# Channel norms of a two-block kernel: sums in four column strips of 128 columns, a reciprocal and a root on 128 columns, and the factor spread by TensorE into PSUM

## The chip, the cores and the metric

One core of one Trainium2 chip runs the whole program. The metric is the device time of one execution in microseconds. The kernel before took 2011.86 us (median of 3 runs, 2007.55 to 2015.01); the profiled execution is one more run, of 2005.91 us, and its span in the profile is 2004.1 us.

## What is computed

Two transformer-like blocks over 512 tokens with 1024 channels, in fp32. The first has a mixer out of a state-space part (SSD) and an RWKV part and a gated feed-forward layer; the second has a modulated mixer of three branches and a hierarchical mixture of experts. The change touches only norms over the channels:

```python
def _rms_norm(x, g):
    xf = x.astype(jnp.float32)
    y = xf * lax.rsqrt(jnp.mean(xf * xf, axis=-1, keepdims=True) + NORM_EPS)
    return (y * g.astype(jnp.float32)).astype(x.dtype)

xn = _rms_norm(h, pre_mix_norm[l]);  proj = xn @ w_in[l]        # pre_mix
y = y.reshape(b, T, SSD_GROUPS, SSD_D // SSD_GROUPS)            # ssd0, ssd1: two groups of 256
y = y * lax.rsqrt(jnp.mean(y * y, axis=-1, keepdims=True) + NORM_EPS)
h = h + _rms_norm(mix, post_mix_norm[l])                        # post_mix
hn = _rms_norm(h, pre_ffn_norm[l])                              # pre_ffn
h = h + _rms_norm(f, post_ffn_norm[l])                          # post_ffn
h = rms_norm(x, g_norm1[l]) * (1.0 + sc1) + sh1                 # sum_1 (second block)
v = layer_norm(v, ln_g, ln_b)                                   # gmlp_var, 512 channels
```

## The kernel before

All activations lie transposed: channels on the 128 partitions, the 512 tokens along the columns, so a row of 1024 channels is eight tiles of 128x512 (`res` is the residual, `xn` the normed one). Every engine has its own program, written out by hand, and semaphores order them; nothing is scheduled by a tool. TensorE's program (from L382) is a list of matmuls in a fixed order. PSUM has eight banks of 512 columns. `open_(what, k, b)` (L392) makes TensorE wait until the former user of bank b has been released, and gives the bank to a new one; `close` tells that it is full; the reader waits with `filled` and releases it with `freed`. So a bank that one reader holds stops TensorE at the next `open_` of this bank, and everything behind that in its program.

A norm over channels takes these steps on three engines:

1. An engine squares each tile (VectorE in pre_mix, ssd, post_mix and gmlp_var, ScalarE in the others), one semaphore count for each.
2. `norm_sum` (L410): one fp32 matmul for each square, a 128x128 block of ones against the tile's 512 columns, all into bank 4. Each of the 128 rows of the result holds the sum over all channels for 512 tokens.
3. `invert_variance` (L1515), on VectorE: `tensor_scalar` from PSUM to `v_tmp` (mean plus epsilon), which releases the bank, then `reciprocal`. Both are 128x512. `v_tmp` and `v_rs` are the halves of the buffer `tiny`.
4. `rstd` on ScalarE (L1151): `Sqrt` of `v_tmp` into `v_rs`, 128x512, recorded at line L1149.
5. VectorE uses `v_rs` as the second tensor of `scalar_tensor_tensor` (the helper `stt`, L1513): tile times gain times factor.

Two functions do step 5 for eight tiles. `scaled_parts` (L1530) makes the input of a projection: `stt` for tile k; ScalarE's `round_hi` (L1170) rounds it into the high part; VectorE subtracts the two for the low part (`in_lo`, `in_ff_lo`), two tiles behind; TensorE's projection begins with tile 0's low part. `add_normed` (L1826) multiplies a tile by gain and factor and adds it to the residual, one tile behind, and ScalarE squares the new residual for the next norm (`squares_of_x`, L1159).

Helpers give the line of many operations: `tt`, `ts` and `stt` are L1507, L1510 and L1513 in the profile, `mm` is L386, `tr` L390.

The places around the norms in TensorE's program: after the "mix" projection (L784) come the sums for post_mix, then `last_modulation(0)`, then the sums for pre_ffn, then the first feed-forward matmuls. `last_modulation` (L469) needs two weight units of 1 MB, a and b: for each, eight matmuls of a 128x32 stationary block, in four column strips of 32, by 256 columns (`rows_of_unit`, L455), an evacuation by ScalarE (`last_mod_rows`), and column matmuls into bank 7. After the feed-forward layer the same follows for post_ffn, `last_modulation(1)` and sum_1. Then two `bias_row` matmuls (L838, 4 output rows by 512 columns, banks 4 and 5), and the "p2" projection of the second block (L840).

Weights come through a ring of two slots (`stream`, L2393): SyncE loads a unit once the unit two before it is used up, which the first instruction on the next unit tells. GpSimd splits each half unit into a high and a low part (L2325 `tensor_scalar`, L2332 `tensor_tensor`), both in SBUF, and waits for the unit's load and for a free slot of the parts.

## Time and profile before

| what | value |
|---|---|
| median of 3 runs | 2011.86 us (2007.55 to 2015.01) |
| the profiled execution, its span | 2005.91 us, 2004.1 us |
| busy: TensorE matmuls, VectorE, ScalarE, GpSimd | 90%, 62%, 24%, 34% |
| TensorE's granted clock, mean of the span | 0.926 of full |
| `reciprocal` on 128x512 in `invert_variance` | 8 times, 26.8 us |
| ScalarE's `Sqrt` on `tiny` | 8 times, 5.0 us |

The rows below have the form: start, duration, engine, line, operation, output<-inputs, shapes, count, and in brackets the idle time before and what ended it. TensorE's fp32 matmuls show as two records each, and a row that merges n records runs from the first start to the last end, so the time from one to the next is less than a record's own length. PE is TensorE, PEld its weight loads, DVE VectorE, ACT ScalarE, POOL GpSimd, SP SyncE.

### The profile page before, as it was taken

The page shows a single profiled execution, that of the slowest core. Times are in us where ns is not written, and L with a number is a line of the kernel's source. Part 1 is how long each engine was busy: PE and PEld are TensorE (multiplying, and loading weights), DVE is VectorE, ACT ScalarE, POOL GpSimd, SP SyncE. Part 2 cuts the span into 40 slices and gives each one's busy share as a digit, 9 for nine tenths or more (in the row PEclk, how much of TensorE's full clock was granted, in tenths as well). Part 3 has the DMA queues.
Part 4 walks back from the last instruction along what each step waited for, and adds up shares of the span by engine and source line. Part 5 has one row for each costly group of instructions (what it writes and reads, how often), then busy time and mean ns, then how long its engine had stood idle before and what let it go on. Part 6 is the DMA issues. An engine that isn't in the chain of part 4 may idle for free.

```text
span 2004.1 us, 28891 instructions
## 1 busy us (share of the span) xinstructions
PE 1805.5 (90%) x11642; PEld 1377.2 (69%) x11642; DVE 1235.2 (62%) x1605; ACT 490.5 (24%) x734; POOL 684.2 (34%) x383
## 2 busy tenths in 40 slices
PE   5999858888969999999889999999898997799998
PEld 4888536766737777777558788876676775566665
DVE  6959366653468888888640385838634544467664
ACT  2121324432021010001221111212143003354443
POOL 2665000001415666666246554005433663000000
PEclk9999679998979999999989999569999999899999
DMA  5221321121114222322212221002311225588884
GB/s 199 86 103 63 117 94 45 51 102 44 64 63 158 90 99 84 104 84 86 82 64 94 79 81 64 1 1 85 100 63 43 85 99 217 200 352 335 321 327 176
DMA packets 34067, 230.49 MB, mean 115 GB/s; under 512 B 4132, under 2 KB 4388, under 8 KB 8232
## 3 DMA queue, kind: packets, MB, share of 16 engines
q1 hardware_dynamic: 30240, 214.48, 29.6%
q10 hardware_dynamic: 2136, 10.24, 1.4%
q0 software_dynamic: 1584, 4.21, 0.6%
q8 instruction: 84, 1.38, 0.3%
q14 instruction: 23, 0.19, 0.0%
HBM read 220.98 MB, written 9.50 MB: 115 GB/s over the span
## 4 chain that ended last, share of the span: by engine, by line
PE 74%; DVE 15%; ACT 4%; DMA 4%; issue 3%; POOL 0%; SPq 0%; DVEq 0%; ACTq 0%; POOLq 0%
PE psum L386 72%; DVE arena L1513 4%; DVE arena L1507 3%; DMA arena<-units 2%; ACT arena L1149 2%; PE psum L390 2%; DVE arena L1510 1%; DVE tiny L1521 1%; ACT L1149 1%; DVE residual L1507 1%; DMA weight_ring<-units 1%; DVE expert_lo L1507 1%; ACT expert_hi L1149 0%; ACT tiny L1149 0%; DMA arena<-x 0%
## 5 line engine op out<-in xcount | busy, mean ns | idle before, releaser
L1149 ACT ACTIVATE arena<-psum 128x512 f32<-128x512 f32 (+4 forms) x295 | 149.3, 521 | 896.2 <-PE psum L386 779.6
L386 PE MATMUL psum<-arena 64*64 64x64 f32 (+5 forms) x2908 | 262.3, 282 | 37.6 <-DVE arena L1507 23.9
L386 PEld LDWEIGHTS psum<-arena 64*64 64x64 f32 (+3 forms) x2908 | 184.4, 166 | 98.3 <-issue 43.9
L386 PE MATMUL psum<-normed_hi,w_in_hi 128*128 128x512 f32 x512 | 205.1, 401 | 12.6 <-DVE in_lo L1507 8.3
L386 PE MATMUL psum<-normed_hi,w_in_lo 128*128 128x512 f32 x512 | 203.5, 397 | 0.0
L386 PE MATMUL psum<-in_lo,w_in_hi 128*128 128x512 f32 x512 | 200.5, 392 | 0.0
L1513 DVE SCALAR_TENSOR_TENSOR arena<-arena,fixed_data 128x512 f32<-128x512 f32 x134 | 188.8, 1409 | 13.5 <-DVE arena L1510 0.2
L1507 DVE TENSOR_TENSOR arena<-arena,psum 128x512 f32<-128x512 f32 (+2 forms) x200 | 110.9, 589 | 134.1 <-PE psum L386 85.5
L2332 POOL TENSOR_TENSOR w_ff_lo<-weight_ring,w_ff_hi 128x1024 fp32r<-128x1024 f32 x66 | 167.0, 2530 | 5.5
L2332 POOL TENSOR_TENSOR w_in_lo<-weight_ring,w_in_hi 128x1024 fp32r<-128x1024 f32 x64 | 163.8, 2560 | 5.3
L386 PE MATMUL psum<-arena,fixed_data 128*128 128x512 f32 (+10 forms) x424 | 135.9, 487 | 30.5 <-DVE arena L1507 20.8
L1507 DVE TENSOR_TENSOR arena<-arena 128x512 f32<-128x512 f32 (+3 forms) x200 | 144.7, 735 | 13.4 <-PE psum L386 5.2
L386 PE MATMUL psum<-normed_hi,w_ff_hi 128*128 128x512 f32 x352 | 139.3, 396 | 8.2 <-DVE in_ff_lo L1507 8.2
L2325 POOL TENSOR_SCALAR w_in_hi<-weight_ring 128x1024 fp32r<-128x1024 f32 x64 | 73.0, 1141 | 203.0 <-PE psum L386 165.1
L2325 POOL TENSOR_SCALAR w_br_hi<-weight_ring 128x1024 fp32r<-128x1024 f32 x44 | 46.6, 1059 | 276.1 <-PE psum L386 159.2
L386 PE MATMUL psum<-in_ff_lo,w_ff_hi 128*128 128x512 f32 x352 | 140.7, 400 | 0.0
L386 PE MATMUL psum<-normed_hi,w_ff_lo 128*128 128x512 f32 x352 | 140.4, 399 | 0.0
L2325 POOL TENSOR_SCALAR w_ff_hi<-weight_ring 128x1024 fp32r<-128x1024 f32 x66 | 74.7, 1132 | 177.1 <-PE psum L386 151.9
L386 PEld LDWEIGHTS psum<-normed_hi,w_in_hi 128*128 128x128 f32 x512 | 96.4, 188 | 42.5 <-issue 14.5
L2325 POOL TENSOR_SCALAR w_out_hi<-weight_ring 128x1024 fp32r<-128x1024 f32 x8 | 8.9, 1112 | 335.2 <-PE psum L386 333.6
L386 PEld LDWEIGHTS psum<-in_lo,w_in_hi 128*128 128x128 f32 x512 | 96.8, 189 | 23.0
L2332 POOL TENSOR_TENSOR w_br_lo<-weight_ring,w_br_hi 128x1024 fp32r<-128x1024 f32 x44 | 110.0, 2499 | 3.7
(226 smaller groups left out, 3564.6 us busy)
## 6 DMA issues: line engine op xcount, KB each, us to landing
weight_ring<-units SPq DMA_DIRECT2D x124, 1024.0 KB, 4.9
arena<-units SPq DMA_DIRECT2D x55, 1024.0 KB, 7.5
normed<-units SPq DMA_DIRECT2D x20, 1024.0 KB, 8.6
slots<-arena ACTq DMA_DIRECT2D x7, 516.0 KB, 5.1
arena<-slots SPq DMA_DIRECT2D x7, 516.0 KB, 5.7
fixed_data<-fixed ACTq DMA_DIRECT2D x1, 2944.0 KB, 12.0
arena<-x SPq DMA_DIRECT2D x4, 512.0 KB, 5.9
arena<-bias_rows ACTq DMA_DIRECT2D x2, 896.0 KB, 5.9
```

The source lines that it names most:

```text
L386: return nc.tensor.matmul(o, l, r, start=start, stop=stop)
L390: return nc.tensor.transpose(o, i, C("ident", k, 0, k))
L1149: return nc.scalar.activation(o, i, func, **kw)
L1507: return V.tensor_tensor(o, a, b, op)
L1510: return V.tensor_scalar(o, a, s1, s2, op0) if op1 is None else V.tensor_scalar(o, a, s1, s2, op0, op1)
L1513: return V.scalar_tensor_tensor(o, a, s1, b, op0, op1)
L1521: V.reciprocal(v_tmp, v_tmp).then_inc(sem("variance_inverted"), 1)
L2325: first = nc.gpsimd.tensor_scalar(hi, raw, 1.0, 1.0, ALU.mult, ALU.mult)
L2332: nc.gpsimd.tensor_tensor(lo, raw, hi.bitcast(F32), ALU.subtract).then_inc(sem("split_ready"), 1)
```

## The change

The sums of steps 2 to 4 are kept on 128 columns instead of 512. `token_sums` replaces `norm_sum` for the eight norms: for each square it does four matmuls of a 128x32 block of ones, one for each quarter j of 128 tokens, which write columns 0 to 127 of PSUM rows 32j to 32j+31. `tensor_scalar`, `reciprocal` and `Sqrt` work on 128x128. `spread_rs` is new on TensorE: it waits for the root and does four 128x128 matmuls, whose stationary block is one column of the identity repeated 128 times, so that row 32j of `v_rs` comes out on all partitions, in columns 128j on; the result is ("rs", what), in bank 4 (5 and 6 for ssd). VectorE's `stt` read it from PSUM, and the last of them releases the bank; what waited for its own semaphore count now waits for this release. In gmlp_var the spread stands one weight unit after the sums, and the two units behind the sums are given one by one. `gmod` is computed ahead of the factor of sum_1 instead of after it. The sums `sum_bonus`, `sum_y` and `gmlp_mean` stay as they were.

```diff
+            def token_sums(what, srcs, ready, b=4):
+
+                o = open_(what, 0, b)
+                for k, src in enumerate(srcs):
+                    pe.wait_ge(*ready(k))
+                    for j in range(4):
+                        last = mm(o[32 * j:32 * j + 32, 0:P], C("ones", P, 0, 32), src[:, j * P:(j + 1) * P],
+                                  k == 0, k == len(srcs) - 1)
+                close(last, what)
+
+            def spread_rs(what, b=4):
+
+                n_rs[0] += 1
+                pe.wait_ge(sem("rstd_ready"), n_rs[0])
+                o = open_(("rs", what), 0, b)
+                for j in range(4):
+                    last = mm(o[:, j * P:(j + 1) * P], C("ident", P, 32 * j, 32 * j + 1).to_broadcast([P, P]), v_rs[:, 0:P])
+                close(last, ("rs", what))
...
-            norm_sum("sum_pre_mix", [A(SQ + k * T) for k in range(KT)], C("ones"), lambda k: (sem("sq_pre_mix"), k + 1))
+            token_sums("sum_pre_mix", [A(SQ + k * T) for k in range(KT)], lambda k: (sem("sq_pre_mix"), k + 1))
+            spread_rs("sum_pre_mix")
...
-            pe.wait_ge(sem("ssd_out_ready"), 4)
+            pe.wait_ge(sem("ssd_out_ready"), 2)
+            for g in range(2):
+                emptied(pe, ("rs", f"sum_ssd{g}"))
...
             sums("sum_post_mix", sq8, "sq_post_mix")
+            spread_rs("sum_post_mix")
             last_modulation(0)
             sums("sum_pre_ffn", sq8, "sq_pre_ffn")
+            spread_rs("sum_pre_ffn")
...
             sums("gmlp_var", [A(g_SQ + k * T) for k in range(4)], "sq_gmlp")
-            project("p2", 2, w_in2, in2, 18)
+            project("p2", 1, w_in2, in2, 18)
+            spread_rs("gmlp_var")
+            project("p2", 1, w_in2, in2, 20)
...
-                f(v_rs, v_tmp, ACT.Sqrt).then_inc(sem("rstd_ready"), 1)
+                f(v_rs[:, 0:P], v_tmp[:, 0:P], ACT.Sqrt).then_inc(sem("rstd_ready"), 1)
...
-                V.tensor_scalar(v_tmp, PSB[bank_of(what, k)], scale, add, ALU.mult, op1).then_inc(freed(what, k), 1)
+                V.tensor_scalar(v_tmp[:, 0:P], PSB[bank_of(what, k)][:, 0:P], scale, add, ALU.mult, op1).then_inc(freed(what, k), 1)
                 emptied(dve, what, k)
-                V.reciprocal(v_tmp, v_tmp).then_inc(sem("variance_inverted"), 1)
+                V.reciprocal(v_tmp[:, 0:P], v_tmp[:, 0:P]).then_inc(sem("variance_inverted"), 1)
...
-                dve.wait_ge(sem("rstd_ready"), n_rstd[0])
+                filled(dve, ("rs", what))
+                return PSB[bank_of(("rs", what))]
...
-                        stt(tiles.raw(k), res[:, k, :], gain(k), v_rs, ALU.mult, ALU.mult).then_inc(sem("scaled"), 1)
+                        stt(tiles.raw(k), res[:, k, :], gain(k), rs, ALU.mult, ALU.mult)\
+                            .then_inc(sem("scaled") if k < KT - 1 else freed(("rs", what)), 1)
...
-                        stt(src(k), src(k), S(gain, k), v_rs, ALU.mult, ALU.mult).then_inc(sem("term_ready"), 1)
+                        stt(src(k), src(k), S(gain, k), rs, ALU.mult, ALU.mult)\
+                            .then_inc(sem("term_ready") if k < KT - 1 else freed(("rs", what)), 1)
```

Three places of TensorE's program show what moves. In the rows, `arena,fixed_data` is squares against ones, `tiny,fixed_data` the spread, `weight_ring,smalls` the rows of a modulation unit. First, the end of the "mix" projection, before:

```order
L386 MATMUL psum<-y_lo,w_out_hi 128x512
L386 MATMUL psum<-arena,fixed_data 128x512 [waits sq_post_mix,bank4_free]
L386 MATMUL psum<-arena,fixed_data 128x512 [waits sq_post_mix] x7
L386 MATMUL psum<-weight_ring,smalls 32x256 [waits bank5_free,weights0_loaded]
L386 MATMUL psum<-weight_ring,smalls 32x256 x7
```

and with the change, from the last of the eight squares on:

```order
L386 MATMUL psum<-arena,fixed_data 32x128 [waits sq_post_mix]
L386 MATMUL psum<-arena,fixed_data 32x128 x3
L386 MATMUL psum<-tiny,fixed_data 128x128 [waits bank4_free,rstd_ready]
L386 MATMUL psum<-tiny,fixed_data 128x128 x3
L386 MATMUL psum<-weight_ring,smalls 32x256 [waits bank5_free,weights0_loaded]
L386 MATMUL psum<-weight_ring,smalls 32x256 x7
```

The spread, which waits for the root, stands ahead of the modulation. Second, sum_1 and the bias rows (`fixed_data 4x512`) ahead of the "p2" projection, before:

```order
L386 MATMUL psum<-arena,fixed_data 128x512 [waits sq_1,bank4_free]
L386 MATMUL psum<-arena,fixed_data 128x512 [waits sq_1] x7
L386 MATMUL psum<-fixed_data 4x512 [waits bank4_free]
L386 MATMUL psum<-fixed_data 4x512 [waits bank5_free]
L386 MATMUL psum<-normed_hi,w_in_hi 128x512 [waits h_ready,bank0_free,split_ready]
```

and with the change, from the last square on:

```order
L386 MATMUL psum<-arena,fixed_data 32x128 [waits sq_1]
L386 MATMUL psum<-arena,fixed_data 32x128 x3
L386 MATMUL psum<-tiny,fixed_data 128x128 [waits bank4_free,rstd_ready]
L386 MATMUL psum<-tiny,fixed_data 128x128 x3
L386 MATMUL psum<-fixed_data 4x512 [waits bank4_free]
L386 MATMUL psum<-fixed_data 4x512 [waits bank5_free]
L386 MATMUL psum<-normed_hi,w_in_hi 128x512 [waits h_ready,bank0_free,split_ready]
```

The wait for bank 4 ahead of the first bias row was one for the `tensor_scalar` of sum_1; now it is one for the last reader of its spread factor. Third, the two ssd norms, with the change:

```order
L386 MATMUL psum<-arena,fixed_data 32x128 [waits sq_ssd,bank6_free]
L386 MATMUL psum<-arena,fixed_data 32x128 x3
L386 MATMUL psum<-arena,fixed_data 32x128 [waits sq_ssd]
L386 MATMUL psum<-arena,fixed_data 32x128 x3
L386 MATMUL psum<-tiny,fixed_data 128x128 [waits bank5_free,rstd_ready]
L386 MATMUL psum<-tiny,fixed_data 128x128 x3
L386 MATMUL psum<-tiny,fixed_data 128x128 [waits bank6_free,rstd_ready]
L386 MATMUL psum<-tiny,fixed_data 128x128 x3
```

Both sums stand ahead of both spreads, each norm in a bank of its own.

## Rows read from the trace of the kernel before

**Rows 1.** The page, part 4: share of the last-ending chain by engine.

```profile
PE 74%; DVE 15%; ACT 4%; DMA 4%; issue 3%; POOL 0%; SPq 0%; DVEq 0%; ACTq 0%; POOLq 0%
```

**Rows 2.** The chain of waits, 555 to 610 us: start, duration, what.

```profile
565.29 3.36 DVE tiny L1521
...
568.67 0.64 ACT tiny L1149
...
569.34 1.42 DVE normed L1513 x2
...
570.75 0.60 DVE residual L1507
571.35 0.66 DVE normed L1513
...
577.86 2.75 DVE residual L1507
...
588.91 0.70 DVE tiny L1519
```

**Rows 3.** The timeline, 557 to 566 us, all engines.

```profile
557.49 7.03 PE L386 MATMUL psum<-arena,fixed_data 128*128 128x512 f32 x16
...
564.45 1.07 PE L386 MATMUL psum<-weight_ring,smalls 128*32 128x256 f32 x16
564.56 0.69 DVE L1519 TENSOR_SCALAR tiny<-psum 128x512 f32<-128x512 f32 x1 [5.55 <-PE psum L386]
```

**Rows 4.** VectorE's groups by form: names, shapes, count, busy us, mean ns, idle.

```profile
L1521 DVE RECIPROCAL tiny<-tiny 128x512 f32<-128x512 f32 x8 | 26.8, 3353 | 0.3
...
L1513 DVE SCALAR_TENSOR_TENSOR arena<-arena,fixed_data,psum 128x512 f32<-128x512 f32 x16 | 11.9, 744 | 10.6 <-ACT arena L1149 6.9 <-PE psum L386 3.1
...
L1513 DVE SCALAR_TENSOR_TENSOR arena<-residual,smalls,tiny 128x512 f32<-128x512 f32 x8 | 5.8, 745 | 0.0
...
L1507 DVE TENSOR_TENSOR arena<-psum,arena 128x128 f32<-128x128 f32 x4 | 1.2, 290 | 5.5 <-PE psum L386 5.5
...
L1807 DVE RECIPROCAL smalls<-smalls 128x32 f32<-128x32 f32 x1 | 0.4, 353 | 0.0
```

**Rows 5.** ScalarE's groups by form.

```profile
L1149 ACT ACTIVATE smalls<-smalls 128x32 f32<-128x32 f32 x2 | 0.5, 229 | 8.7 <-DVE smalls L1807 5.1 <-DVE smalls L1999 3.6
```

**Rows 6.** The timeline of TensorE, 1156.5 to 1176 us.

```profile
1157.37 0.39 PE L386 MATMUL psum<-fixed_data 128*128 128x128 f32 x2
...
1157.82 0.39 PE L386 MATMUL psum<-fixed_data 128*128 128x128 f32 x2
```

**Rows 7.** The timeline, 562 to 608 us: modulation unit b, its columns, GpSimd's first split.

```profile
569.93 1.93 PE L386 MATMUL psum<-weight_ring,smalls 128*32 128x256 f32 x16 [4.40 <-DMA weight_ring<-units]
...
571.79 1.87 PE L386 MATMUL psum<-smalls,arena 128*128 128x1 f32 x8
...
576.14 1.18 POOL L2325 TENSOR_SCALAR w_ff_hi<-weight_ring 128x1024 fp32r<-128x1024 f32 x1 [25.22 <-DMA weight_ring<-units]
```

**Rows 8.** Windows: busy us of PE, PEld, DVE, ACT, POOL, granted clock, DMA share, GB/s.

```profile
26.00:28.00 2.00, 0.00 (x0) 0.00 (x0) 2.00 (x1) 0.00 (x0) 0.00 (x0) 1.00 0.00 0
...
573.00:586.00 13.00, 9.46 (x17) 4.00 (x17) 12.47 (x12) 4.04 (x7) 7.95 (x4) 0.76 0.42 153
```

**Rows 9.** The timeline, 8 to 46 us: pre_mix's squares and its `tensor_scalar`.

```profile
12.12 10.72 DVE L1507 TENSOR_TENSOR arena<-residual 128x512 f32<-128x512 f32 x8 [12.12 <-ACT residual L1149]
...
25.16 0.69 DVE L1519 TENSOR_SCALAR tiny<-psum 128x512 f32<-128x512 f32 x1 [2.23 <-PE psum L386]
```

**Rows 10.** The timeline, 1015 to 1033 us: bias rows, eighth `stt`, evacuation of tile 0.

```profile
1015.50 3.58 PE L386 MATMUL psum<-fixed_data 128*4 128x512 f32 x4 [0.78 <-DVE tiny L1519]
...
1027.69 0.74 DVE L1513 SCALAR_TENSOR_TENSOR arena<-residual,smalls,tiny 128x512 f32<-128x512 f32 x1
...
1032.07 0.60 ACT L1149 ACTIVATE arena<-psum 128x512 f32<-128x512 f32 x1
```

**Rows 11.** The chain of waits, 985 to 1035 us, its last piece.

```profile
1029.15 6.02 PE psum L386 x25
```

More of the change, by code:

```diff
@@ L587, in _ @@
             for g in range(2):
-                norm_sum(f"sum_ssd{g}", [A(s_XD + (2 * g + i) * T) for i in range(2)], C("ones"),
-                         lambda i: (sem("sq_ssd"), 2 * g + i + 1))
+                token_sums(f"sum_ssd{g}", [A(s_XD + (2 * g + i) * T) for i in range(2)],
+                           lambda i: (sem("sq_ssd"), 2 * g + i + 1), 5 + g)
+            for g in range(2):
+                spread_rs(f"sum_ssd{g}", 5 + g)
             def gram(what, m, banks, l, r, crossed=False):
@@ L1266, in _ @@
                 rstd()
-            act.wait_ge(sem("ssd_out_ready"), 4)
+            act.wait_ge(sem("ssd_out_ready"), 2)
+            for g in range(2):
+                emptied(act, ("rs", f"sum_ssd{g}"))
             act.wait_ge(sem("sigmoid_ready"), 1)
@@ L1905, in _ @@
             acc = lambda k: A(F_ACC + k * T)
-            rstd("sum_post_ffn", 1.0 / D, 1e-6)
-            add_normed(acc, "g_post_ffn")
-            def modulated(tiles, scale_at, shift_at, gain, name):
-                link(stt(gmod[:, :], mod[:, scale_at:scale_at + KT], 1.0, S(gain, 0, KT), ALU.add, ALU.mult))
-                scaled_parts(tiles, lambda k: gmod[:, k:k + 1], name, lambda k: mod[:, shift_at + k:shift_at + k + 1])
+            rs = rstd("sum_post_ffn", 1.0 / D, 1e-6)
+            add_normed(acc, "g_post_ffn", "sum_post_ffn", rs)
             last_mod(1)
-            rstd("sum_1", 1.0 / D, 1e-6)
-            modulated(in2, 8, 0, "g1", "h_ready")
+            link(stt(gmod[:, :], mod[:, 8:8 + KT], 1.0, S("g1", 0, KT), ALU.add, ALU.mult))
+            rs = rstd("sum_1", 1.0 / D, 1e-6)
+            scaled_parts(in2, "sum_1", rs, lambda k: gmod[:, k:k + 1], "h_ready", lambda k: mod[:, k:k + 1])
             filled(dve, "w_s")
@@ L1928, in _ @@
                 tt(A(g_SQ + k * T), p2(AV + k), p2(AV + k), ALU.mult).then_inc(sem("sq_gmlp"), 1)
-            rstd("gmlp_var", 1.0 / T, 1e-6)
+            rs = rstd("gmlp_var", 1.0 / T, 1e-6)
             for k in range(4):
                 v = p2(AV + k)
-                link(stt(v, v, S("gmlp_g", k), v_rs, ALU.mult, ALU.mult))
+                last = stt(v, v, S("gmlp_g", k), rs, ALU.mult, ALU.mult)
+                if k < 3:
+                    link(last)
+                else:
+                    last.then_inc(freed(("rs", "gmlp_var")), 1)
+                    emptied(dve, ("rs", "gmlp_var"))
                 ts(v, v, S("gmlp_b", k), None, ALU.add).then_inc(sem("gmlp_v_ready"), 1)
```

50 lines of the change are left out of this document (30 added, 20 removed).

## The prediction

> **What bounds the kernel now.** I read the page first. The chain that ended last is mostly TensorE; VectorE's share is much smaller [rows 1]. TensorE bounds the long projections, and time is to be had only where it stands still for a short serial piece. The chain of waits, cut to the stretch after the "mix" projection, shows such a piece [rows 2]: a norm runs its sums, `tensor_scalar`, `reciprocal`, `Sqrt`, then the first operation that reads the factor. From 564.56 (`tensor_scalar`) [rows 3] to 569.34 that is 4.78 us, one instruction at a time. Seven of the eight norms lie so on the chain; only `gmlp_var` runs beside a projection. So 7 x 4.78 = 33 us are exposed, plus the ends of the sums, and a part of this is what the change can take directly.
>
> **Costs of the pieces.** The reciprocal takes 3353 ns for 512 columns and 353 ns for 32 [rows 4]: 6.25 ns a column on a base of 153, so 953 ns for 128. A VectorE operation on 128 columns from PSUM takes 290 ns [rows 4], against 0.69 us of the `tensor_scalar` on 512 [rows 3]. `Sqrt`: 0.64 us for 512 [rows 2], 229 ns for 32 [rows 5], so 310 ns for 128. With three handoffs of 0.04 us the chain up to the root is 0.29 + 0.95 + 0.31 + 0.12 = 1.67 us. New behind it is the spread, four fp32 matmuls of 128x128 by 128. Where such matmuls stand in a row, every second one begins 0.45 us after the last but one [rows 6]: 0.223 us each, 0.89 us for four, at the full clock. At half the clock the same work takes about twice as long (a modulation unit: 1.07 us [rows 3] and 1.93 us [rows 7]). The granted clock is still 1.00 (2.4 GHz) between 26 and 28 us, with TensorE idle since 25 [rows 8], and the idle time ahead of a spread is now under 2 us; so I take 0.89 where TensorE was busy before (pre_mix, post_mix, post_ffn) and 1.79 where it worked thinly (both ssd norms, pre_ffn, sum_1). With 0.1 us of handoff the whole chain is 2.66 or 3.56 us: it saves 2.1 us three times and 1.2 us four times.
>
> The strip sums are 32 small matmuls in place of 8 large ones. The old ones are 16 records in 7.03 us [rows 3], 0.86 us per square. The nearest row for the new is the modulation unit: eight matmuls into four strips of 32, 256 columns each, 16 records in 1.07 us [rows 3], so strips run beside each other. That is 0.13 us a matmul at most, and by columns half of it for 128. I take 0.07: 0.28 us a square, 2.2 us for eight. Bounds: 0.053 (a quarter of 0.21) and 0.13; twice that at half the clock.
>
> The 44 `stt` that now read the factor from PSUM: 744 ns with a PSUM operand, 745 ns with `tiny` [rows 4]. I cost them at nothing. The Trainium skill (VectorE: DVE Perf Modes, the section on the TRN2 errata) states 120 fixed cycles for a PSUM source against 58 from SBUF, which speaks against this change; as an estimate from that page it would add 65 ns to each, 2.9 us in all. By that rule the 744 would be about 810, so the trace does not agree.
>
> **Place by place.**
> *pre_mix*: eight squares run from 12.12 to 22.84, `tensor_scalar` starts at 25.16, since the sums lag [rows 9]. Now they end about 0.5 us after the last square, 1.85 earlier. With the chain: 3.95 us.
> *ssd0, ssd1*: here VectorE is late, not the sums: 2 x 1.2 = 2.4 us. The separate banks 5 and 6 add nothing.
> *gmlp_var*: TensorE does 16 small matmuls (1.1 us) and a spread (0.9) for 4 x 0.86 us of sums: 1.45 us off a stretch that TensorE bounds. The factor is there only after one more weight unit; a second unit, as long, still covers VectorE's eight operations. Nothing lost.
> *post_mix and pre_ffn*: the sums begin at 557.49 and the last square ends at 559.01, where VectorE's 5.55 us of idle time begin [rows 3]. Now they end near 559.8: 4.8 us earlier. The chain's 2.1 brings the first `stt` to 562.5 instead of 569.34. `add_normed` took 16 us, because from 576.14 on GpSimd splits weights [rows 7], 7.95 us of work [rows 8], and VectorE's sums of two SBUF tensors stretch from 0.6 to 2.75 us [rows 2]. Undisturbed it is 8 x (0.66 + 0.60) + 0.1 = 10.2 us. The splits hang on the weight ring: modulation unit a must begin (now after the spread, 562.6 instead of 564.45), 5.5 us later unit b (564.45 to 569.93), 6.2 us later GpSimd: 574.3. So `add_normed` ends at 572.7, clear of it. ScalarE's squares wait for the rows of unit b (570.4) and at 0.64 us each end at 575.5. TensorE's sums use bank 4, which now the eighth `stt` frees (571.4), no later than the modulation columns end (571.79 + 1.87 before [rows 7], 571.8 now), and keep up with the squares. `tensor_scalar` starts at 575.9 instead of 588.91: 13.0. Chain: 1.2. GpSimd is now busy from 574.3 to 582 and meets the reciprocal and the first roundings, but the first three `stt` read PSUM and cover it mostly: minus 0.5. Together **13.7 us**.
> *post_ffn and sum_1*: the same pattern, 13.6 us up to the first `stt`. But here the change adds a wait. The two `bias_row` matmuls ran in the shadow of the reciprocal (1015.50, 3.58 us) [rows 10]. They open bank 4, which is now free only after the eighth `stt` of `scaled_parts`, and the whole "p2" projection is queued behind them on TensorE. Before, the eighth `stt` ends at 1028.43 and ScalarE takes tile 0 at 1032.07, 3.64 us later [rows 10]. Now 3.58 us of bias rows follow it (TensorE idle for 9 us, so at 1.2 GHz like before), then 24 matmuls at 0.24 [rows 11] and 0.4 while the clock rises: 9.7 us. Loss **6.1 us** (bounds: 3.9 if all is at the full clock, 10.5 if tile 0 is at the half). Left: 7.5.
> Sum: 3.95 + 2.4 + 1.45 + 13.7 + 7.5 = 29.0. The profiled execution took 2005.91 us (span 2004.1 and 1.8 around it) and would take 1977; the median shown, 2011.86, is 6 above it, and against that I expect **1983**. About 0.5% (10 us) is what a measurement of this kernel can tell from no change.
>
> **Rivals.**
> *A, the collision only moves.* The 2 x 5.9 us that `add_normed` loses to GpSimd are not saved but fall, all but 0.5 each that I have counted, on the reciprocal and on the roundings of `scaled_parts`. For it: GpSimd's 8 us now lie across that phase. Against it: only the subtractions there read two SBUF tensors, and they begin 7 us after GpSimd. It gives 29.0 - 10.8 = 18: 1994.
> *B, the bias rows cost less.* If TensorE keeps the full clock there and in the four spreads that I have at half, it is 2.2 + 3.6 us more: 1977. The 3.58 us for two matmuls of 512 columns [rows 10], twice the 0.86 each of rows 3, speak against it.
> *C, slower: the strips run one after another.* A 128-column matmul then costs 0.223 us at the full clock or 0.45 at the half, whatever its strip. The sums stand on TensorE ahead of every `tensor_scalar`, and in pre_ffn and sum_1 cannot begin before bank 4 is free. At 0.223 the sums win nothing, the chains' 7 to 8 us are left and the bias rows take 6.1: 2010. At 0.45, post_mix comes 7 us later than now and pre_ffn adds 14 us behind the eighth `stt`: minus 9 us there, minus 15 with sum_1, minus 4 in pre_mix and ssd: 2040. In the mean 2025; it decides from about 0.23 us a matmul on. The 1.07 us of the modulation unit speak against it [rows 3]: serial, they would be 3.4.
> *D, little effect*: the stages are held by the ring. Unit b comes 5.5 us behind a whatever VectorE does. If all later steps hung on it, pre_ffn and sum_1 would come only 1.9 us earlier each, plus 2.4 of chains; with 7.8 from pre_mix, ssd and gmlp that is 16, less 6.1 for the bias rows: 2002.
>
> **How the numbers follow.** Forecast 0.60, A 0.18, B 0.10, C 0.04, D 0.08. The range runs from B with the strips at their lower bound (1972) to A with the bias rows' upper bound (1998); it leaves out C, D and little of the rest. Faster by over 0.5% (below 2001.8): forecast, A, B and some of D, 0.90. Within 0.5%: most of D and the mild end of C, 0.07. Slower: 0.03, the rest of C.
>
> **What would show it.** The reciprocal at 0.95 us eight times and the root at 0.31; 4.78 us down to 2.7 or 3.6; strip records in bunches of 0.3 us a square; four matmuls from `tiny` in 0.9 or 1.8 us; `add_normed` at 10.2 us twice with GpSimd's first split behind it; bias rows that start with the end of the eighth `stt`, and tile 0 9.7 us after it; the `stt` still at 745 ns. I would be wrong if the strips take 0.2 us each, if the `stt` from PSUM grow, or if the subtractions of `scaled_parts` are now the ones stretched to 2.7 us.

## The result, and the profile after

The changed kernel takes 1986.12 us (median of 4 runs, 1984.23 to 1987.32), the kernel before 2009.70 us (4 runs on the same chip, 2004.48 to 2015.01): a ratio of 0.987, 95% interval 0.9843 to 0.9896. It is faster by 1.3%, as forecast; 1983 was predicted, with 1972 to 1998 as the range. The profiled execution took 1986.03 us, its span is 1984.1 us, and its mean granted clock 0.915 (2004.1 us and 0.926 in the profile of before).

VectorE's groups by form, answering to [rows 4] (`stt` is L1550 now, `tensor_scalar` L1556, `reciprocal` L1558):

```profile
L1550 DVE SCALAR_TENSOR_TENSOR arena<-arena,fixed_data,psum 128x512 f32<-128x512 f32 x32 | 23.5, 742 | 29.1 <-PE psum L386 20.5 <-ACT arena L1181 8.0
L1550 DVE SCALAR_TENSOR_TENSOR arena<-residual,fixed_data,psum 128x512 f32<-128x512 f32 x16 | 11.5, 738 | 4.1 <-PE psum L386 4.1
L1558 DVE RECIPROCAL tiny<-tiny 128x128 f32<-128x128 f32 x8 | 7.6, 953 | 0.3
...
L1550 DVE SCALAR_TENSOR_TENSOR normed<-normed,fixed_data,psum 128x512 f32<-128x512 f32 x8 | 5.9, 742 | 1.6 <-PE psum L386 1.6
...
L1556 DVE TENSOR_SCALAR tiny<-psum 128x128 f32<-128x128 f32 x8 | 2.3, 290 | 24.7 <-PE psum L386 24.7
```

The reciprocal at 953 ns and the `tensor_scalar` at 290 are the predicted numbers to the nanosecond, and the `stt` (738 to 743 ns) that read the factor from PSUM are not slower than the 745 ns of before.

The timeline of the two norms behind the "mix" projection, answering to [rows 2, 3, 7] (weight loads, evacuations and repeats left out):

```profile
556.60 1.95 PE L386 MATMUL psum<-arena,fixed_data 128*32 128x128 f32 x64
557.34 0.69 DVE L1544 TENSOR_TENSOR arena<-normed 128x512 f32<-128x512 f32 x1 [4.75 <-ACT normed L1181]
558.62 0.29 DVE L1556 TENSOR_SCALAR tiny<-psum 128x128 f32<-128x128 f32 x1 [0.59 <-PE psum L386]
558.95 0.95 DVE L1558 RECIPROCAL tiny<-tiny 128x128 f32<-128x128 f32 x1
559.93 0.31 ACT L1181 ACTIVATE tiny<-tiny 128x128 f32<-128x128 f32 x1 [2.63 <-DVE tiny L1558]
...
560.30 1.16 PE L386 MATMUL psum<-tiny,fixed_data 128*128 128x128 f32 x8 [1.74 <-ACT tiny L1181]
...
561.49 1.41 DVE L1550 SCALAR_TENSOR_TENSOR normed<-normed,fixed_data,psum 128x512 f32<-128x512 f32 x2 [1.59 <-PE psum L386]
...
566.82 1.94 PE L386 MATMUL psum<-weight_ring,smalls 128*32 128x256 f32 x16 [4.36 <-DMA weight_ring<-units]
...
570.38 1.28 DVE L1544 TENSOR_TENSOR residual<-residual,normed 128x512 f32<-128x512 f32 x2
...
570.51 3.64 PE L386 MATMUL psum<-arena,fixed_data 128*32 128x128 f32 x64
...
572.83 1.04 POOL L2369 TENSOR_SCALAR w_ff_hi<-weight_ring 128x1024 fp32r<-128x1024 f32 x1 [22.89 <-DMA weight_ring<-units]
...
574.22 0.29 DVE L1556 TENSOR_SCALAR tiny<-psum 128x128 f32<-128x128 f32 x1 [2.49 <-PE psum L386]
...
575.90 1.16 PE L386 MATMUL psum<-tiny,fixed_data 128*128 128x128 f32 x8 [1.74 <-ACT tiny L1181]
577.09 2.07 DVE L1550 SCALAR_TENSOR_TENSOR arena<-residual,fixed_data,psum 128x512 f32<-128x512 f32 x3 [1.59 <-PE psum L386]
...
579.08 1.22 DVE L1544 TENSOR_TENSOR in_ff_lo<-arena,normed_hi 128x512 fp32r<-128x512 f32 x1
```

Read it from the top. The strips (the sums in four column strips) do 32 matmuls in 1.95 us, 0.06 each, where the eight full sums took 7.03; VectorE idles 0.59 us behind its last square instead of 5.55. From `tensor_scalar` (558.62) to the first `stt` (561.49) it is 2.87 us instead of 4.78. `add_normed` ends at 571.7, 10.2 us long, and GpSimd's first split begins at 572.83, behind it. The first subtraction of `scaled_parts` is the only one that meets GpSimd (1.22 us).

The same place at the second block's entrance, answering to [rows 10]:

```profile
986.68 0.29 DVE L1556 TENSOR_SCALAR tiny<-psum 128x128 f32<-128x128 f32 x1 [2.78 <-PE psum L386]
...
988.36 2.08 PE L386 MATMUL psum<-tiny,fixed_data 128*128 128x128 f32 x8 [1.81 <-ACT tiny L1181]
...
998.40 0.74 DVE L1550 SCALAR_TENSOR_TENSOR arena<-residual,smalls,psum 128x512 f32<-128x512 f32 x1
...
999.20 3.58 PE L386 MATMUL psum<-fixed_data 128*4 128x512 f32 x4 [8.76 <-DVE arena L1550]
```

The bias rows stood at 1015.50, waiting for the `tensor_scalar` of `tiny`; now they wait 8.76 us and are released by the eighth `stt`. ScalarE takes tile 0 at 1009.44, 10.3 us behind this `stt` (3.64 before).

To see where time is gained and given back, I lined up ScalarE's 668 activations (the program has the same ones in the same order) and took how much earlier each starts than before:

| up to | before minus after, us | of this place | predicted |
|---|---|---|---|
| pre_mix: first rounding | 2.4 | 2.4 | 3.95 |
| ssd heads (no change there) | -2.8 | -5.2 | 0 |
| ssd0, ssd1 | -0.9 | 1.9 | 2.4 |
| end of "mix" (no change) | 1.0 | 1.9 | 0 |
| post_mix, pre_ffn: first rounding | 16.6 | 15.6 | 13.7 |
| end of the feed-forward layer | 15.3 | -1.3 | 0 |
| post_ffn, sum_1: first rounding | 29.3 | 14.0 | 13.6 |
| tile 0 of p2 | 22.6 | -6.6 | -6.1 |
| tile 1 of p2 | 22.1 | -0.5 | 0 |
| gmlp_var | 23.4 | 1.3 | 1.45 |
| the last activation (no change) | 20.05 | -3.4 | 0 |

The ssd heads are counted up to ssd0's `tensor_scalar`. The norms, with what follows from them at the feed-forward layer and at the first tiles of p2, give 26.8 us together (29.0 predicted); the other three places, whose instructions are the same, take 6.7 of it away. The largest of these is the ssd heads, where the granted clock (the third number from the end, 1.00 is 2.4 GHz) differs between the two profiles. First before, then after, the window from 225 to 315 us:

```profile
225.00:315.00 90.00, 60.91 (x507) 39.33 (x509) 46.65 (x81) 30.64 (x48) 0.00 (x0) 0.72 0.25 87
```

```profile
225.00:315.00 90.00, 62.25 (x514) 42.18 (x515) 39.94 (x77) 29.57 (x47) 0.00 (x0) 0.58 0.25 83
```

Whether this clock is the change's doing or differs from one execution to the next is the first question for the runs.

### The profile page after: what moved, and what is told of

It reads as the page before. It is cut to its first block, busy times and chain, and to the rows that moved or that the text cites. A ratio compares the mean times of both kernels' runs of the same rounds, so it can differ in the third digit from the quotient of the medians.

```text
span 1984.1 us, 29596 instructions
## 1 busy us (share of the span) xinstructions
PE 1787.9 (90%) x11994; PEld 1387.9 (70%) x11994; DVE 1200.4 (61%) x1605; ACT 486.5 (25%) x734; POOL 680.5 (34%) x383
## 4 chain that ended last, share of the span: by engine, by line
PE 76%; DVE 12%; DMA 5%; ACT 4%; issue 3%; POOL 0%; SPq 0%; DVEq 0%; ACTq 0%; POOLq 0%
PE psum L386 74%; DVE arena L1550 3%; DVE arena L1544 3%; DMA arena<-units 2%; ACT arena L1181 2%; DMA weight_ring<-units 1%; PE psum L390 1%; DVE arena L1547 1%; ACT L1181 1%; DVE expert_lo L1544 1%; DMA normed<-units 1%; ACT expert_hi L1181 0%; DMA arena<-x 0%; DVE tiny L1558 0%; POOL slots L2420 0%
## 5 line engine op out<-in xcount | busy, mean ns | idle before, releaser
L386 PE MATMUL psum<-arena 64*64 64x64 f32 (+5 forms) x2908 | 266.6, 285 | 42.9 <-DVE arena L1544 29.1
L1550 DVE SCALAR_TENSOR_TENSOR arena<-arena,fixed_data 128x512 f32<-128x512 f32 x134 | 187.5, 1399 | 13.5 <-DVE arena L1547 0.2
L1544 DVE TENSOR_TENSOR arena<-arena 128x512 f32<-128x512 f32 (+3 forms) x200 | 144.7, 735 | 14.2 <-PE psum L386 6.1
L386 PE MATMUL psum<-arena,fixed_data 128*32 128x128 f32 (+11 forms) x712 | 96.4, 374 | 19.7 <-DVE arena L1544 19.2
L386 PEld LDWEIGHTS psum<-in_lo,w_in_hi 128*128 128x128 f32 x512 | 97.0, 190 | 22.1
L386 PEld LDWEIGHTS psum<-normed_hi,w_in_lo 128*128 128x128 f32 x512 | 96.9, 189 | 21.7 <-issue 0.5
```

The lines of the kernel that those rows point to most:

```text
L386: return nc.tensor.matmul(o, l, r, start=start, stop=stop)
L1544: return V.tensor_tensor(o, a, b, op)
L1550: return V.scalar_tensor_tensor(o, a, s1, b, op0, op1)
```

## The experiments

All edits are to the changed kernel unless said otherwise. Ratios are to the kernel before on the same chip.

**The changed kernel again.**

> The changed kernel once more, nothing edited. It measures how far one execution of it stands from the next in the same profile rows, above all the granted clock between 200 and 310 us (the ssd heads), where the first profile of it had half the clock from 233.6 to 308.7 us and the kernel before full clock for parts of it. Theory (the 3 to 5 us missing there are a varying clock, not the change): the half-clock stretch lies elsewhere or has another length this time, and the shift of ScalarE's instructions there differs by microseconds. Rival (the change causes it, by the separate banks and the spreads): the half clock stands again from about 234 to 309 us. Time 1986, within 4.

1990.15 us (6 runs, 1983.87 to 1991.96), ratio 0.9892 (0.9862 to 0.9922). The shifts at the norms repeat within 0.3 us of the first profile. The half-clock stretch stood again from 236 to 311 us, which speaks for the rival; so the kernel before had to be looked at again.

**The kernel before again.**

> The kernel before once more, for a second look at its granted clock. All four profiles of kernels with the change show half the clock from about 234 to 309 us nearly without a break (75 us), the first profile of the kernel before only in pieces there (about 36 us of it), and it was, at a mean clock of 0.926, one of its quick executions. Theory (a varying clock, and the first profile of before was an untypical one): this profile shows half the clock for 60 us or more between 230 and 310 us, and a mean clock of about 0.919. Rival (the change sets off the long half-clock stretch): again only 30 to 45 us in pieces.

2007.71 us (one run). The heads ran at half the clock for 73 of the 90 us:

```profile
225.00:315.00 90.00, 63.25 (x334) 39.39 (x334) 41.80 (x69) 28.25 (x44) 0.00 (x0) 0.59 0.24 85
```

The theory holds as far as it goes: 0.59 with the old norms against 0.58 with the new, so the change is not needed for the long half-clock stretch. Over the twelve profiles of this study the heads, up to ssd0's `tensor_scalar`, take 90.2 us (54 of them at half the clock) to 98.9 us (about 80 at half), and neither end is bound to the old or the new norms: the kernel before has 91.5 and 98.9, the changed one 96.7 and 98.9, and 90.2 is the run with the factor copied, below. A single profile of this kernel therefore carries 5 us and more of luck there, and the -5.2 in the table can be of that kind. What two profiles of before cannot show is how often each form comes: the six profiles whose program is that of the changed kernel up to there all lie between 96.4 and 98.9 us, so whether the change makes the short form rarer stays open. A second such place is the stretch from the last evacuations of RWKV to the end of "mix" (415 to 558 us of the first profile), also without a changed instruction: 142.8 and 143.3 us in the two profiles of before, 142.8 to 149.9 in the ten others; whether the change has a part in that is open too. This profile shows a second thing: post_ffn and sum_1 took 22.3 us from post_ffn's root to the first rounding, where the first profile took 25.7, since less of GpSimd's splits met `add_normed` (14.0 us long here, 16.1 there). The gain of that place, counted from the end of the feed-forward layer, is 10.7 us against this profile and 14.0 against the first.

**Bias rows in other banks.**

```diff
-                close(mm(open_("bias_row", i, 4 + i)[0:4, :], S("rel_bias", 0, 4), C("bucket", P, i * T, (i + 1) * T)),
+                close(mm(open_("bias_row", i, 5 + i)[0:4, :], S("rel_bias", 0, 4), C("bucket", P, i * T, (i + 1) * T)),
```

> The two bias rows go to banks 5 and 6 instead of 4 and 5, so nothing of them waits for the spread factor's last reader. Theory (they stand on the path because of bank 4 alone, 6.1 us predicted and 6.6 read from the shift of tile 0): they run at about 991 us, right behind the spread and beside the first roundings, tile 0 is evacuated about 3.6 us after the eighth scalar_tensor_tensor instead of 11, and the time falls by 6 to 7 us, to 1979.5. Rival 1 (the p2 projection is bound by something else right behind, such as the split weights): the tile comes earlier but the time falls by under 2 us. Rival 2 (the two matmuls only move onto other work): no change, 1986.

1978.50 us (6 runs, 1967.28 to 1988.90), ratio 0.9835 (0.9794 to 0.9876). Timeline around the eighth `stt`:

```profile
991.59 3.58 PE L386 MATMUL psum<-fixed_data 128*4 128x512 f32 x4
...
999.63 0.74 DVE L1550 SCALAR_TENSOR_TENSOR arena<-residual,smalls,psum 128x512 f32<-128x512 f32 x1
...
1004.00 0.60 ACT L1181 ACTIVATE arena<-psum 128x512 f32<-128x512 f32 x1
```

The two matmuls run right behind the spread with no wait, and tile 0 comes 3.6 us behind the eighth `stt`. From the first rounding to tile 0 it is 11.46 us instead of 18.13, 6.7 less; to tile 1 it is 7.2 less, and none of that is lost up to 1244 us. The medians differ by 11.6; what is above 7.2 is not of this place. The mean clock ran from 0.911 to 0.926 over these six runs (0.911 to 0.915 beside them), which goes with the rest but is not shown to be all of it. So the one wait that the change added is worth 6.7 us at tile 0 and 7.2 in all, it needed no bank in common, and both rivals fall.

**Modulation unit a ahead of the spread.**

```diff
             sums("sum_post_mix", sq8, "sq_post_mix")
+            rows_of_unit(N_MOD1 + 0, W_MOD2_UNITS[0], 5)
             spread_rs("sum_post_mix")
...
-                for j in range(2):
-                    rows_of_unit(N_MOD1 + 2 * g + j, W_MOD2_UNITS[g] + j, 5 + j)
+                rows_of_unit(N_MOD1 + 2 * g + 1, W_MOD2_UNITS[g] + 1, 6)
```

(the same for post_ffn)

> The first modulation unit's eight matmuls stand ahead of the spread instead of behind it, in post_mix and in post_ffn. They then run beside the reciprocal and the root (1.07 us in 1.7 us of waiting) and the load of unit b is free to start about 2.8 us earlier. Theory (GpSimd's splits hang on the ring, and vector sums of two SBUF tensors stretch beside them): unit b and GpSimd come 2.7 us earlier, so GpSimd starts near 570 and meets the last one or two additions of add_normed (0.68 us each, up to 2.75 us beside GpSimd); ScalarE's squares, which wait for unit b's rows, gain 2.7 us but are held by add_normed's end. In all between 2 us faster and 2 us slower over both places: 1986, with the last one or two additions at 1 to 2.75 us. Rival 1 (the ring sets the place, no collision): both places gain 2.7 us, 1980.5. Rival 2 (the collision takes it all and more): 3 us lost twice, 1992.

1986.46 us (6 runs, 1985.42 to 1992.95), ratio 0.9884 (0.9854 to 0.9914): no gain. The timeline shows the collision of before come back at the end of `add_normed` (not the one of rival A, which is with the reciprocal and the roundings behind it):

```profile
575.50 1.05 POOL L2370 TENSOR_SCALAR w_ff_hi<-weight_ring 128x1024 fp32r<-128x1024 f32 x1 [20.24 <-DMA weight_ring<-units]
575.70 4.16 DVE L1545 TENSOR_TENSOR residual<-residual,normed 128x512 f32<-128x512 f32 x2
...
576.63 2.68 POOL L2377 TENSOR_TENSOR w_ff_lo<-weight_ring,w_ff_hi 128x1024 fp32r<-128x1024 f32 x1
```

GpSimd begins 11.6 us after the `tensor_scalar` of the norm instead of 14.2, meets the last two additions, and they take 4.16 us instead of 1.28. From the root of post_mix to the first rounding of pre_ffn it is 20.4 us instead of 17.9 to 18.2, a loss, of which later work hides most; 0.9 of it is pre_ffn's spread, which ran at half the clock this time (2.05 us instead of 1.16). Between post_ffn's root and the first rounding behind sum_1 nothing is gained or lost. The place of the spread, ahead of unit a, is what keeps `add_normed` clear: it is part of the gain, by 1.2 us of room.

**Three reciprocals.**

```diff
+                for _ in range(2):
+                    link(V.reciprocal(v_tmp[:, 0:P], v_tmp[:, 0:P]))
                 V.reciprocal(v_tmp[:, 0:P], v_tmp[:, 0:P]).then_inc(sem("variance_inverted"), 1)
```

> The reciprocal is done three times in a row on the same 128 columns (an odd number gives the same value), 1.9 us more in each of the eight norms. Theory (seven of eight norms lie bare on the path, gmlp_var does not, and GpSimd's start moves along since unit a stands behind the spread): 7 x 1.9 = 13.4 us more, 1999.5. Rival (where the ring of weights sets the pace, the two places with modulation units absorb part): 7 us or less, 1993.

2007.60 us (12 runs, 1999.07 to 2016.61), ratio 0.9982 (0.9961 to 1.0004), 17.5 us above the unedited kernel. At pre_mix the shift is 2.1 us, in each ssd norm 2.0, at post_mix 2.0, none in gmlp_var: so seven chains are bare. But post_mix and pre_ffn together lost 7.9 us instead of 3.9, and post_ffn and sum_1 5.5, of which 2 are made good later: with TensorE idle for longer, the spread of post_mix and unit a ran at half the clock (2.07 and 1.94 us instead of 1.16 and 1.07) and unit b came 6.5 us after its load was issued instead of 4.8. The mean clock of these runs is 0.901 to 0.911, of the unedited ones beside them 0.911 to 0.915. By the medians a microsecond on these chains costs 1.3, not 1 (17.5 us for 7 x 1.9).

**The full sums back, the rest narrow.**

```diff
-                    for j in range(4):
-                        last = mm(o[32 * j:32 * j + 32, 0:P], C("ones", P, 0, 32), src[:, j * P:(j + 1) * P],
-                                  k == 0, k == len(srcs) - 1)
+                    last = mm(o, C("ones"), src, k == 0, k == len(srcs) - 1)
...
-                V.tensor_scalar(v_tmp[:, 0:P], PSB[bank_of(what, k)][:, 0:P], scale, add, ALU.mult, op1).then_inc(freed(what, k), 1)
+                for j in range(4):
+                    r = slice(32 * j, 32 * j + 32)
+                    last = V.tensor_scalar(v_tmp[r, 0:P], PSB[bank_of(what, k)][r, j * P:(j + 1) * P], scale, add, ALU.mult, op1)
+                last.then_inc(freed(what, k), 1)
```

> The strip sums are undone: one 128x512 matmul for each square, as before, and four tensor_scalars of 32x128 that read the four diagonal blocks; reciprocal, root and spread stay on 128 columns. Theory (the sums' tail was worth as much as predicted): post_mix and post_ffn lose 5.0 us each (first tensor_scalar 5.5 instead of 0.6 us behind the last square), pre_ffn and sum_1 3 us at the full clock to 10 at the half, pre_mix 1.4, gmlp_var 2.4, and the three further tensor_scalars, 0.3 us each, 0.9 in seven norms, 6 us: 26 to 40 us in all, about 2018. Rival (the sums ran beside other work and the gain was the shorter reciprocal and root): under 15 us, 2002 or less.

2017.59 us (10 runs, 2011.58 to 2023.87), ratio 1.0043 (1.0018 to 1.0069): slower than the kernel before. Three lines of its timeline give the reason:

```profile
565.72 7.03 PE L386 MATMUL psum<-arena,fixed_data 128*128 128x512 f32 x16
...
572.79 1.19 DVE L1556 TENSOR_SCALAR tiny<-psum 32x128 f32<-32x128 f32 x4 [5.55 <-PE psum L386]
...
585.78 9.68 PE L386 MATMUL psum<-arena,fixed_data 128*128 128x512 f32 x16
```

The 5.55 us of idle time of before are back, and pre_ffn's sums, which cannot begin before the eighth `stt` frees bank 4, last 9.68 us. By the aligned activations: pre_mix 1.9, the two ssd norms 0.9, post_mix 5.9, pre_ffn 8.0, post_ffn 6.1, sum_1 7.9, gmlp_var 2.2, together 33 us of which 0.6 is made good later: within the 26 to 40 expected. In this form, with 0.9 us more for the four `tensor_scalar` in each norm, the shorter reciprocal and root do not pay for the spread and the wait for bank 4; the strips do.

**Factor copied into SBUF.**

```diff
                 filled(dve, ("rs", what))
-                return PSB[bank_of(("rs", what))]
+                link(ts(v_tmp, PSB[bank_of(("rs", what))], 1.0, None, ALU.mult))
+                return v_tmp
```

(and a wait, ahead of each norm, for the last reader of `v_tmp`, which was passed long before)

> VectorE first copies the spread factor from PSUM into SBUF (a tensor_scalar of 128x512), and the scalar_tensor_tensor read it from there; the bank is still released by the last of them, so the order of the work stays. All pay for the copy, 0.69 + 0.04 us in seven bare norms: 5.1 us. Theory 1 (an operand in PSUM keeps the first operations of scaled_parts clear of GpSimd, whose splits lie beside them in pre_ffn and sum_1 now): the first two to four of them there, now 0.66 us apart, stretch towards 2.7 us, 3 to 8 us more over both places: 1996 to 2001. Theory 2 (where the operand lies makes no difference): each stays at 0.74 us and the time is 5 us up, 1993. A fixed cost of a PSUM source would show as scalar_tensor_tensor under 0.74 us now.

1992.47 us (9 runs, 1986.28 to 1999.00), ratio 0.9925 (0.9900 to 0.9950). Timeline of VectorE at pre_ffn, then the tile view of the same operations, in which the three numbers are least, median and most ns:

```profile
575.53 0.69 DVE L1547 TENSOR_SCALAR tiny<-psum 128x512 f32<-128x512 f32 x1 [1.59 <-PE psum L386]
...
576.26 3.81 DVE L1550 SCALAR_TENSOR_TENSOR arena<-residual,fixed_data,tiny 128x512 f32<-128x512 f32 x3
```

```profile
L1550 DVE SCALAR_TENSOR_TENSOR arena<-residual,fixed_data,tiny x3: 740/740/2486, 576.3 to 579.3; 128x512 f32<-128x512 f32 x3
```

One of the three takes 2486 ns beside GpSimd's split, where with the factor in PSUM the three took 2.07 us in all; in sum_1 they take 2.43 instead of 2.06. So the mechanism of theory 1 is there, but its size is not: 1.7 and 0.4 us, 2.1 together where it had 3 to 8, and only one operation stretched in pre_ffn where it had two to four. The median is the 1993 of theory 2: the time alone does not tell 5 us from 7, and the rows decide. The Trainium skill (SBUF — State Buffer, the section "Who interferes with whom") says that a VectorE instruction with two SBUF inputs contends with a GpSimd instruction that reads SBUF, and one with at most one (outside the modes in which it takes both ports) does not; these rows agree. Away from GpSimd the operand's place makes no difference: `stt` of `normed` by the factor take 742 ns from PSUM and 747 from `tiny`.

```profile
L1550 DVE SCALAR_TENSOR_TENSOR normed<-normed,fixed_data,tiny 128x512 f32<-128x512 f32 x8 | 5.9, 747 | 0.0
```

**The ssd norms as a pair, with the bias rows in banks 5 and 6.**

```diff
             for g in range(2):
-                rs = rstd(f"sum_ssd{g}", 1.0 / 256, 1e-6)
+                invert_variance(f"sum_ssd{g}", 1.0 / 256, 1e-6, q=g * P)
+            for g in range(2):
+                filled(dve, ("rs", f"sum_ssd{g}"))
+                rs = PSB[5 + g]
```

(`q` is the first column in `v_tmp` and `v_rs`, for the root and the spread too)

> Two edits: the bias rows in banks 5 and 6, as in the run of that alone, and the two ssd norms taken as a pair: both tensor_scalars and reciprocals first, the second in columns 128 to 255, then both roots and spreads, then the four scalar_tensor_tensor. Theory (VectorE waits 2.5 us in each ssd norm for root and spread, and the second wait can lie beside the first pair of products): the stage ends about 3 us earlier, and with the bias rows 6.6 the time is 9 to 10 us under that of the change, about 1977 to 1979 (by the median of 1988 over both sets of runs). Rival (the RWKV stage behind it is held by something else): only the bias rows' part, 1982.

1979.32 us (6 runs, 1974.06 to 1980.45), ratio 0.9849 (0.9813 to 0.9885). In the ssd norms:

```profile
291.66 0.23 DVE L1556 TENSOR_SCALAR tiny<-psum 128x128 f32<-128x128 f32 x1
...
292.14 3.78 PE L386 MATMUL psum<-tiny,fixed_data 128*128 128x128 f32 x16 [0.87 <-ACT tiny L1181]
```

Both spreads run back to back, and from the first `tensor_scalar` to the operation behind the fourth `stt` it is 6.8 us instead of 10.2. The 3.4 us are not seen at the end of "mix" in this profile: between 425 and 551 us, in the second place of luck named above, it lost as much, as the unedited kernel's second profile did (3.1). The time alone doesn't tell it from the bias rows.

**The same kernel once more.**

> The bias rows in banks 5 and 6 and the ssd norms as a pair, unedited, beside the run with TensorE kept busy, and for a second measurement. Ratio to the kernel before 0.985 again, within 0.003; ssd norms 3.4 us shorter than with the change alone, tile 0 of p2 6.6 us earlier against the last norm, both to within 0.2 us in the profile. If they are, the remaining scatter of the total is the granted clock elsewhere, above all in the ssd heads (91.5 to 103 us so far).

1978.18 us (6 runs, 1966.08 to 1983.45), ratio 0.9821 (0.9790 to 0.9852). The ssd norms are 3.4 us shorter again. From sum_1's first rounding to tile 0 it is 12.3 us, 5.8 less than with the change alone and not 6.6: the expectation of 0.2 us was too narrow, as 2.6 us of half clock lay there this time, 0.1 in the run before.

**TensorE kept busy.** The same kernel with matmuls that nobody reads:

```diff
+            def fill(n, b, src=C("bucket", P, 0, T)):
+
+                for _ in range(n):
+                    mm(PSB[b], C("ones"), src, True, True)
...
                 rows_of_unit(N_MOD1 + 2 * g, W_MOD2_UNITS[g], 5)
+                fill(5, 0)
                 rows_of_unit(N_MOD1 + 2 * g + 1, W_MOD2_UNITS[g] + 1, 6)
...
+            fill(1, 0)
             spread_rs("sum_pre_ffn")
```

(in pre_mix one behind the second square's strips, two behind the third's, two ahead of the spread; one ahead of the spread of sum_1)

> On top of the same kernel, TensorE gets matmuls whose result nobody reads (128x128 by 512 columns, 0.86 us each at the full clock) where it stood idle around the norms: three among pre_mix's sums and two ahead of its spread, five between modulation unit a and unit b in both places, one ahead of the spreads of pre_ffn and sum_1. Theory (TensorE's granted clock falls to half after those idle stretches, and that is why pre_mix's spread takes 2.08 us, the sums of pre_ffn and sum_1 3.64 and unit b 1.94): the clock stays full there, pre_mix's and sum_1's spreads take 1.16 us, 0.9 less each, the sums of pre_ffn and sum_1 end about 1.2 us earlier each, their columns and unit b take 1 us: 4 to 5 us in all, 1974.5 against 1979. Rival 1 (the clock falls all the same, or falls elsewhere for it): 1979, with rows as before. Rival 2 (the idle matmuls stand in the way of unit b or of the spreads, at half clock 1.8 us each): slower, 1982.

1974.86 us (5 runs, 1971.01 to 1979.72), ratio 0.9824 (0.9800 to 0.9847), 3.3 us under the kernel beside it by the medians and not under it by the ratios (0.9824 and 0.9821), so the times show no gain; the rows carry the verdict. The window of the first 60 us of the changed kernel and of this one, then the timeline of this one:

```profile
0.00:60.00 60.00, 41.66 (x219) 32.36 (x220) 43.74 (x51) 16.12 (x25) 23.39 (x20) 0.89 0.47 184
```

```profile
0.00:60.00 60.00, 44.73 (x235) 31.95 (x236) 44.97 (x52) 16.13 (x25) 23.82 (x20) 1.00 0.46 184
```

```profile
23.47 0.29 DVE L1567 TENSOR_SCALAR tiny<-psum 128x128 f32<-128x128 f32 x1 [0.54 <-PE psum L386]
...
25.15 1.16 PE L386 MATMUL psum<-tiny,fixed_data 128*128 128x128 f32 x8
...
978.25 1.07 PE L386 MATMUL psum<-weight_ring,smalls 128*32 128x256 f32 x16
979.25 1.18 PE L386 MATMUL psum<-smalls,arena 128*128 128x1 f32 x8
...
986.22 1.16 PE L386 MATMUL psum<-tiny,fixed_data 128*128 128x128 f32 x8 [0.76 <-ACT tiny L1192]
987.30 1.88 PE L386 MATMUL psum<-fixed_data 128*4 128x512 f32 x4
```

The clock stays full, pre_mix's spread takes 1.16 us instead of 2.08, and unit b in post_ffn 1.07 instead of 1.94; sum_1's spread takes 1.16 instead of 2.08 and 2.07 in the changed kernel and the pair's first profile, but it took 1.16 in the pair's second one too. Against the two profiles of the kernel without them, pre_mix gains 0.9 to 1.1 us, post_mix with pre_ffn 0.5 to 0.7, post_ffn with sum_1 2.1 to 2.6: 3.5 to 4.4 in all, at and under the low end of the 4 to 5 expected, and 0.5 to 1.3 of it is given back before tile 0. By these rows both rivals fall. Pre_ffn falls short because its sums still ran half at the low clock.

## Why the prediction was right, point by point

The forecast held, by its own mechanism: 26.8 us at the places against 29.0 (3.3 less by the second profile of before), and rivals A, C and D are out. That the total lies 3 us from the forecast is in part luck: pre_mix came 1.5 us short and post_mix with pre_ffn 1.9 over, and profile against profile the forecast was 1977 and the measured time 1986.03, since the places that no instruction of the change touches took 6.7 us away. The 6 us added for the median, because the profile of before was a quick execution, cover that. C by the strips' 0.06 us (it needed 0.23), D by 15.6 and 14.0 us where it had about 3 each, A by the timeline: GpSimd lies on the reciprocal and the first three `stt`, of which neither stretches, and one subtraction pays 0.5 us, as counted. The run with unit a first shows how near the old collision is (1.2 us), and the copied factor that A's own mechanism exists: with both tensors in SBUF the first `stt` do stretch, by 2.1 us over both places. B falls with the bias rows at 3.58 us; its other half, the clock at the spreads, was right in one of four.

*Term by term.*
- The reciprocal, root and `tensor_scalar` came out as worked from their rows. The `stt` at nothing: shown by 742 against 747 ns, and against the 65 ns more that each would cost by the estimate from the Trainium skill (VectorE: DVE Perf Modes, the section on the TRN2 errata). What was not in the sum: PSUM also keeps the first of them in pre_ffn and sum_1 clear of GpSimd, worth 2.1 us by the copied factor.
- The strips were mis-sized on the safe side, 0.06 for 0.07 us a matmul.
- The spread takes 1.16 or 2.08 us as a record, and the first `stt` begins 1.19 or 2.11 us after its start, where 0.99 and 1.89 were in the sum: 0.2 us too little in each norm. Which clock it would find was wrong in two of seven: pre_mix at half, where full was assumed, and pre_ffn at full, where half was.
- **pre_mix**, 3.95 predicted, 2.4 measured, is the term that failed. "Now they end about 0.5 us after the last square, 1.85 earlier": VectorE waits 0.77 us for them where it waited 2.23 [rows 9], and its `tensor_scalar` starts 1.36 earlier. The reason is the same as for the spread: the clock fell at 22 us instead of 30. The strips need less of TensorE than the sums did, it waits up to 2.33 us between squares, and it goes on at half the clock:

```profile
20.59 0.43 PE L386 MATMUL psum<-arena,fixed_data 128*32 128x128 f32 x8 [2.33 <-DVE arena L1544]
...
23.80 0.29 DVE L1556 TENSOR_SCALAR tiny<-psum 128x128 f32<-128x128 f32 x1 [0.77 <-PE psum L386]
...
25.48 2.08 PE L386 MATMUL psum<-tiny,fixed_data 128*128 128x128 f32 x8 [1.83 <-ACT tiny L1181]
```

With TensorE kept busy VectorE waits 0.54 us for the strips and the place gives 3.6 us: the sum's terms were right within 0.4 us for a clock that the change itself took away.
- post_mix with pre_ffn: 15.6 for 13.7; the root of post_mix came 7.8 us earlier relative to the end of "mix" (sums, `tensor_scalar` and reciprocal), and the rest is `add_normed` and pre_ffn's spread at the full clock. 1.3 to 1.6 us of it are given back by the end of the feed-forward layer, in each profile of the changed kernel.
- post_ffn with sum_1: 14.0 against one profile of before, 10.7 against the other, for 13.6. That the collision with GpSimd has a size of its own in each execution was missing from the prediction.
- The bias rows: 6.1 predicted, 6.6 at tile 0 and 7.1 at tile 1 in the shift, 6.7 and 7.2 when undone. The mechanism (a bank whose release moved from an early reader to a late one, with a whole projection queued behind) is shown by the edit.
- gmlp_var 1.3 for 1.45, ssd 1.9 for 2.4.
- Three sums of the prediction do not come out of its own terms. D is 2 x 1.9 + 2.4 + 7.8 = 14.0 earlier and not 16, so 2004. The bias rows' upper bound with tile 0 at half the clock is 3.58 + 24 x 0.48 - 3.64 = 11.5 and not 10.5, which puts the end of the range at 1999. And the "7 to 8 us" of chains in C are given without a working; the chains of the sum itself come to 3 x 2.1 + 4 x 1.2 = 11.1. None of the three changes which of the rivals the runs leave.

*The base.* I took the 6 us between the profile shown and the median as a constant. It goes with the clock: over 17 runs of the kernel before on one chip, mean clock and time run from 0.928 and 1999.35 us to 0.915 and 2018.69 us, some 1.2 us for each 0.001 (0.7 and 1.8 on two other chips, so roughly), and the profile shown was at 0.926 where most runs are near 0.920. The changed kernel's runs are at 0.911 to 0.918. Part of that lies at the norms (13.7 us at half in the first 60 us instead of 6.8) and is in the 26.8 already. That the heads' clock differs between executions is shown for the kernel before; how much of it is chance in the changed one, and why it falls there at all, stays open. Of the 3.4 us behind gmlp_var, 1.4 lie in one short stage of small matmuls (1243 to 1268 us of the profile of before). It takes 24.3 to 24.4 us in both profiles of before, with the full sums and with TensorE kept busy, and 25.8 to 26.5 in the other eight. So these 1.4 us come with the strips wherever TensorE is not kept busy, and are hardly chance, though no run was made for them. The rest is open; the other profiles of kernels with the change take 1 to 6 us less from tile 0 to the end.

## What to carry to other kernels

When a norm's factor is computed on a quarter of the columns, look first at the sums: with 32-row strips side by side they took 1.95 us for 7.03, and without them (and with four `tensor_scalar` in each norm) the narrower reciprocal did not even pay for the spread. When a PSUM bank gets a second, longer-lived user, list what opens that bank next on TensorE: two small matmuls with a whole projection behind them cost 6.7 to 7.2 us, and a different bank number gave it back. And a change that leaves TensorE less to do can drop its clock for the work that follows; a term priced at the clock of before has to be priced at the other level too.

## What the runs showed of the hardware that was not expected

- The same ssd heads, with the same instructions, take 90.2 to 98.9 us, following the time at half the clock (54 to 81 us).
- A microsecond of added VectorE work on the bare chains cost 1.3 us by the medians; beside it a spread and a modulation unit fell to half the clock and the next weight load took 1.7 us longer to its first use.
- Matmuls that nobody reads held TensorE at 2.4 GHz over the first 60 us (window clock 1.00 against 0.89), and the real work behind them took less time (pre_mix's spread 1.16 us instead of 2.08).
- A two-operand VectorE operation beside GpSimd takes 2486 ns with both tensors in SBUF (once in three; the others 740), and three of them 2.07 us in all with one in PSUM.

The lowest median of the study is that of the kernel with the bias rows in banks 5 and 6, the ssd norms as a pair and TensorE kept busy: 1974.86 us, 11 to 15 us under the change itself (1986.12 and 1990.15 in its two sets, which did not run beside it) and 1.8% under the kernel before. By its ratio (0.9824) it cannot be told from the same kernel without the idle matmuls (0.9821).
